# Expert weights in pieces of 2 MB, with runs of 16 KB a partition, in a ring of eight places

## What is computed

```python
x = x + merged(rmsnorm(x, g_mix)) @ w_out            # HGRN2 and pooling, gated; 14 column chunks of w_in
h = rmsnorm(x, g_ffn)
logits = h @ w_router + b_router                     # 32 experts, the top 4 of each token
for e in range(32):                                  # for the tokens sent to expert e
    gate = min(h_e @ w_gate[e] + b_gate[e], 7)
    up = clip(h_e @ w_up[e] + b_up[e], -7, 7)
    y_e = ((up + 1) * gate * sigmoid(1.702 * gate)) @ w_down[e] + b_down[e]
x = x + sum over the experts of weight * y_e
x = x + sigmoid(rmsnorm(x, g_ple) @ w_ple_gate) * (p @ w_ple_proj)
y = rmsnorm(x, g_final)
```

## Time and profile before

| what | value |
|---|---|
| median of three runs | 1386.6 us (1386.1 to 1389.21) |
| the profiled execution's own time | 1386.59 us |
| its span, first to last instruction | 1384.9 us |
| mean granted TensorE clock | 0.982 of full speed |
| PE busy | 1331.2 us (96%) |
| PEld busy | 621.5 us (45%) |
| DVE, ACT, POOL busy | 332.9, 186.4 and 68.3 us |
| DMA queue of SyncE | 442.56 MB (of 10^6 bytes), 77.9% of 16 engines |
| expert pieces issued | 3 x 128, 1024 KB each |

### The profile page before, as it was taken

One profiled execution on the slowest core, in us unless ns is written; L12 is line 12 of the kernel. 1 busy time (PEld: TensorE's weight loads), 2 busy tenths in 40 slices (PEclk: granted clock), 3 DMA queues, 4 the chain that ended last, 5 costly groups with the idle time before them and its releaser, 6 DMA issues.

```text
span 1384.9 us, 15843 instructions
## 1 busy us (share of the span) xinstructions
PE 1331.2 (96%) x6272; PEld 621.5 (45%) x6272; DVE 332.9 (24%) x633; ACT 186.4 (13%) x359; POOL 68.3 (5%) x145
## 2 busy tenths in 40 slices
PE   6999999999899999999999999999999999999995
PEld 5754557364434334343443434434344343434342
DVE  2423424122411221212212122121221212221133
ACT  3314311112111000110001000010000100100022
POOL 7021120030000000000000000000000000000000
PEclk9999999999789999999999999999999999999998
DMA  9743272252559999999999999999999999999920
GB/s 335 264 134 123 61 281 114 62 223 88 215 232 421 421 422 422 421 422 422 422 422 422 422 422 422 422 422 422 422 422 422 422 422 422 422 422 422 420 116 32
DMA packets 79264, 458.70 MB, mean 331 GB/s; under 512 B 8457, under 2 KB 9633, under 8 KB 30080
## 3 DMA queue, kind: packets, MB, share of 16 engines
q1 hardware_dynamic: 73376, 442.56, 77.9%
q0 software_dynamic: 4448, 14.98, 3.5%
q10 hardware_dynamic: 1408, 0.73, 0.2%
HBM read 452.35 MB, written 6.35 MB: 331 GB/s over the span
## 4 chain that ended last, share of the span: by engine, by line
PE 82%; DMA 10%; SPq 3%; DVE 3%; ACT 1%; issue 1%; POOL 0%; ACTq 0%; DVEq 0%
PE bank L965 39%; PE bank L629 10%; PE bank L930 10%; DMA arena<-in_w_up_dram 10%; PE bank L822 4%; PE bank L670 3%; PE bank L1006 3%; SPq L426 3%; PE bank L652 1%; PE bank L742 1%; PE bank L759 1%; PE bank L981 1%; DVE arena L1592 1%; PE bank L939 1%; PE bank L1010 1%; PE bank L598 1%
## 5 line engine op out<-in xcount | busy, mean ns | idle before, releaser
L965 PE MATMUL bank<-arena 128*64 128x512 f32 x3072 | 669.3, 594 | 12.1 <-DVE arena L1592 6.4
L965 PEld LDWEIGHTS bank<-arena 128*64 128x64 f32 x3072 | 226.2, 137 | 442.2 <-issue 438.3
L930 PE MATMUL bank<-arena 128*128 128x128 f32 (+1 forms) x816 | 157.3, 323 | 0.0
L629 PE MATMUL bank<-arena 128*128 128x512 f32 x320 | 144.2, 604 | 0.0
L930 PEld LDWEIGHTS bank<-arena 128*128 128x128 f32 (+1 forms) x816 | 120.6, 201 | 45.4 <-issue 18.0
L629 PEld LDWEIGHTS bank<-arena 128*128 128x128 f32 x320 | 59.8, 192 | 74.3 <-issue 73.5
L1600 DVE TENSOR_TENSOR arena<-bank,arena 128x512 f32<-128x512 f32 (+1 forms) x96 | 61.5, 682 | 96.3 <-PE bank L1006 96.1
L1578 DVE TENSOR_SCALAR arena<-bank 128x512 f32<-128x512 f32 x32 | 20.6, 686 | 195.4 <-PE bank L965 195.4
L1594 DVE COPY arena<-bank 128x512 f32<-128x512 f32 x16 | 11.1, 692 | 217.0 <-PE bank L965 217.0
L670 PE MATMUL bank<-arena 128*128 128x264 f32 x256 | 59.1, 395 | 3.2 <-DVE arena L1328 2.6
L1584 DVE TENSOR_SCALAR arena<-bank 128x512 f32<-128x512 f32 x32 | 20.6, 686 | 168.5 <-PE bank L965 168.5
(11 more groups left out here) (234 smaller groups left out, 736.9 us busy)
## 6 DMA issues: line engine op xcount, KB each, us to landing
arena<-in_w_gate_dram SPq DMA_DIRECT2D x128, 1024.0 KB, 25.5
arena<-in_w_up_dram SPq DMA_DIRECT2D x128, 1024.0 KB, 25.4
arena<-in_w_down_dram SPq DMA_DIRECT2D x128, 1024.0 KB, 21.4
arena<-in_w_in_dram SPq DMA_DIRECT2D x14, 2048.0 KB, 11.5
out_dram<-arena POOLq DMA_DIRECT2D x11, 512.0 KB, 3.8
arena<-in_state_hgrn_dram POOLq DMA_DIRECT2D x8, 512.0 KB, 14.8
arena<-in_w_out_dram SPq DMA_DIRECT2D x4, 1024.0 KB, 14.4
arena<-in_w_ple_gate_dram SPq DMA_DIRECT2D x4, 1024.0 KB, 26.3
```

Source lines behind the costliest of these rows:

```text
L629: ins = pe.matmul(job_bank(name)[:, :], hT[:, k, toks(t)], w[:, k, :], start=(k == 0), stop=(k == KD - 1))
L930: ins = pe.matmul(XG[c][:, (k % 4) * P:(k % 4 + 1) * P], h2[lanes(t), t, every_other(k)], oh[lanes(t), t, :], start=(t == 0), stop=(t == N ...
L965: ins = pe.matmul(out[c][hp(one), :], src[:, k * P + CAP * one:k * P + CAP * one + CAP], w[one][:, j, halves(c)], start=(first and k == 0) ...
```

## The change

A piece becomes half of a matrix, 512 rows, 2 MB. A partition holds four neighbouring rows of the matrix, one run of 16 KB. The ring has eight places and covers the same 16 MB of SBUF. A pair has 12 pieces. A step of `products` waits for two pieces of 2 MB and runs 16 matmuls (32 passes); it frees its places at its end. The slices of `h2` and of the activation have step 4 (16 bytes). Before the loop `granule_used` is counted up by every second `dT` product (4) and by 4 transposes of `h2T`. `w_ple_gate` comes in two loads of 2 MB, still with runs of 4 KB. The diff, cut to its core:

```diff
-GRAN = 2048
+GRAN = 4096
 NGRAN = 3 * D * D // (P * GRAN)
-RING = 16
+RING = 8
...
         gran = [view(R + g * GRAN if g < NGRAN else HG + (g - NGRAN) * GRAN, GRAN).rearrange(
-            "p (j n) -> p j n", j=2) for g in range(RING)]
+            "p (j n) -> p j n", j=4) for g in range(RING)]
...
-            parts = [w.rearrange("o e (g p j) n -> (o e) g p j n", j=2, p=P) for w in (w_gate, w_up, w_down)]
-            ple = w_ple_gate[0].rearrange("(g j p) n -> g p j n", j=2, p=P)
+            parts = [w.rearrange("o e (g p j) n -> (o e) g p j n", j=4, p=P) for w in (w_gate, w_up, w_down)]
+            ple = w_ple_gate[0].rearrange("(g j p) n -> g p j n", j=4, p=P)
...
                     for m in range(3):
-                        for g in range(4):
+                        for g in range(2):
                             for one in range(2):
-                                at_ = 2 * NGRAN * n + 8 * m + 2 * g + one
+                                at_ = 2 * NGRAN * n + 4 * m + 2 * g + one
...
-                pe.matmul(o[:, 0:144], u[:, 0, cc], band0[g], start=True, stop=True, skip_group_check=True).then_inc(s_used, 1)
+                ins = pe.matmul(o[:, 0:144], u[:, 0, cc], band0[g], start=True, stop=True, skip_group_check=True)
+                if c % 2 == 0:
+                    ins.then_inc(s_used, 1)
...
-            turn_rows("h2T", h2, h2_ready, n_used=7, tiles=(2,))
-            turn_rows("h2T", h2, h2_ready, n_used=1, tiles=(0,))
+            turn_rows("h2T", h2, h2_ready, n_used=4, tiles=(2,))
+            turn_rows("h2T", h2, h2_ready, tiles=(0,))
...
             def every_other(k):
-                first = 2 * P * (k // 2) + k % 2
-                return slice(first, first + 2 * P - 1, 2)
+                first = 4 * P * (k // 4) + k % 4
+                return slice(first, first + 4 * P - 3, 4)
...
-                    for g in range(4):
-                        if m == 2 and g % 2 == 0:
-                            pe.wait_ge(s_aTs, 2 * i + g // 2 + 1)
-                        if m == 0 and g == 2:
+                    for g in range(2):
+                        if m == 2:
+                            pe.wait_ge(s_aTs, 2 * i + g + 1)
+                        if m == 0 and g == 1:
                             pe.wait_ge(s_xe, 2 * i + 2)
                         w = list(granules(m, g))
-                        for j in range(2):
-                            k = 2 * g + j
+                        for j in range(4):
+                            k = 4 * g + j
...
-                                    if j == 1 and c == 1 and not (g == 3 and one == 1):
+                                    if j == 3 and c == 1 and not (g == 1 and one == 1):
                                         ins.then_inc(s_used, 1)
```

More of the change, by code:

```diff
@@ L225, in build @@
         wpool = view(G12, 2048).rearrange("p (g k n) -> p g k n", g=4, k=2)
-        wout = view(R + 8 * GRAN, 8192).rearrange("p (k n) -> p k n", k=KD)
+        wout = view(R + 4 * GRAN, 8192).rearrange("p (k n) -> p k n", k=KD)
         band0 = [view(BAND + g * 144, 144) for g in range(4)]
@@ L442, in _ @@
                 load_experts(PER * q, 2 * PER * q)
-            sp.wait_ge(s_used, NGRAN * NE + 4)
+            sp.wait_ge(s_used, NGRAN * NE + 2)
             load_ple()
@@ L446, in _ @@
             with sp.If(more > 0):
-                sp.wait_ge(ld["ple"], 64)
+                sp.wait_ge(ld["ple"], 32)
                 with sp.Fori(1, NBLK) as b:
@@ L450, in _ @@
                         load_experts(b * PAIRS + PER * q, 2 * PER * q)
-                sp.wait_ge(s_used, NGRAN * NE * NBLK + 4)
+                sp.wait_ge(s_used, NGRAN * NE * NBLK + 2)
                 load_ple()
@@ L808, in weights @@
             def weights(w, k, half):
-                return gran[k // 2][:, k % 2, halves(half)] if w is None else w[:, k, halves(half)]
+                return gran[k // 4][:, k % 4, halves(half)] if w is None else w[:, k, halves(half)]
             def quarter(w, k, n):
-                return gran[k // 2][:, k % 2, cols(2, n)] if w is None else w[:, k, cols(2, n)]
+                return gran[k // 4][:, k % 4, cols(2, n)] if w is None else w[:, k, cols(2, n)]
             def product(tag, t, src, w, slices=KD):
@@ L948, in granules @@
                     for one in range(2):
-                        turn, place = divmod(2 * NGRAN * n + 8 * m + 2 * g + one, RING)
+                        turn, place = divmod(2 * NGRAN * n + 4 * m + 2 * g + one, RING)
                         pe.wait_ge(s_gr[place], i0 * (16 * 2 * NGRAN // RING) + 16 * (turn + 1))
@@ L1032, in _ @@
                             pair(b * PAIRS + PER * q, n)
-                pe.wait_ge(ld["ple"], 128)
+                pe.wait_ge(ld["ple"], 64)
             keep_warm(8, Y[1])
@@ L1038, in _ @@
             turn_rows("h3T", h3, lambda t: (s_rows, t + 7))
-            pe.wait_ge(ld["ple"], 64)
+            pe.wait_ge(ld["ple"], 32)
             for t in range(NT):
```

## The result

The changed kernel takes 1544.65 us (median of four runs, 1541.79 to 1546.61) against 1386.6 us for the kernel before (median of three runs, 1386.1 to 1389.21); the ratio of the means is 1.1133, 95% interval 1.1105 to 1.116. A fourth run of the kernel before took 2835.38 us and is left out of these figures. The profiled execution took 1541.79 us, span 1540.0, mean granted clock 0.907 instead of 0.982. The forecast was 1486 us with a range up to 1498, so it had the sign and the place, and was 58.7 us too low.

A forecast was written before the change was run, and what follows sets the result against it. TensorE was taken to set the pace until the ring's lead is eaten, then the weight stream. Kernel before 1386.6, slower loads +105.9 and +1.1, stream waits -7.0: 1486.6 us; full price of the step 1465 to 1498, range 1400 to 1498.

The forecast's parts named there:

- What bounds the kernel, and the place: In the loop, TensorE at 64.7 us a pair outlasts the stream's 59.6 and no longer waits for weights.
- The price of the gather's load: In the gather, a weight load with a step of 16 bytes takes 236 ns instead of 118; chance 0.68.
- The rival with 177 ns: Partial price: a load takes half as much again, a pair 61.4 us, the kernel 1433 us; chance 0.14.
- the upper bound: Each 16 bytes of SBUF touched has its own price: 236 ns a gather load, against a lower bound of 118.
- The transposes' term: The 8 transposes of a pair: each load grows from 120 to 240 ns, adding 8 x 0.120 us a pair.
- the forecast 2.1: Sign of being right: the row of 8 transposes grows from 1.2 to 2.1 us.
- the sum: Kernel before 1386.6, plus 105.9 for 16 pairs, 1.1 for gathers before the loop, less 7.0 of stream waits: 1486.6 us.
- The coarse pieces: First release and last landing each cost 3.5 us, +7.0 us where the stream sets the end; hidden in the forecast.
- The stream's rate: Runs of 16 KB move weights at 428 GB/s instead of 422, 58.8 us a pair; no effect on the forecast time.
- The rule on lines of 16 bytes: SBUF reads need two hits on a 16-byte line; by it the old step is free, the new one not; no price given.
- C: Theory of the follow-up runs, not the prediction: the clock falls because the slow gather gives the array too little work.

The follow-up runs named there:

- step4_turn: The kernel before with step 4 (16 bytes) in the 8 transposes of a pair alone, the gather keeping step 2; 1388.94 us.
- pieces2mb_step2: The changed kernel with each 2 MB piece as two runs of 8 KB a partition, so the slices keep step 2; 1394.73 us.
- narrow32: The kernel before, step 2, with each gather load followed by 32 columns instead of 128; 1402.86 us.
- no8_long: The changed kernel, its gather without the 8 sample rows and with each remaining load and product twice (32 passes of 128 rows); 1476.81 us.
- rows64: The changed kernel with 64 rows instead of 8 in the short passes of the gather; 1539.7 us.
- grouped8: The changed kernel with the gather's loops exchanged, so two changes of row count in a gather instead of eight; 1478.16 us.
- fill256: The changed kernel with each gather load followed by 256 columns instead of 128; 1537.93 us.
- contig_2mb: The changed kernel, but VectorE writes h2 and the activation sorted by slice, so every load is contiguous; 1383.77 us.
- contig_2mb_grouped: The kernel contig_2mb with the gather's loops exchanged as in grouped8, all outputs computed; 1371.16 us.

## Why the prediction missed

**What bounds the kernel, and the place: right.** TensorE sets the end, the gather is what grew, and no products wait for DMA in the loop.

**The price of the gather's load: right.** 233 ns measured for 236 forecast, 48 x (0.233 - 0.118) = 5.5 us a pair. The rival with 177 ns has fallen. The working had luck, though. It chose the upper bound by the single loads of the transposes (140 ns contiguous, 209 with 8 bytes), and just those do not follow it: they stay at 209 ns where I forecast 330.

**The transposes' term (8 x 0.120 = 0.96 us a pair): wrong.** At full clock it is nothing (1.23 us for 1.22, `step4_turn`). The 1.98 us in the changed kernel, which look like the forecast 2.1, are the lower clock. A sign that agrees in size can have another cause; the window's granted clock (0.50) tells them apart.

**The failed step is the sum** "1386.6 + 105.9 + 1.1 - 7.0 = 1486.6 us": it took every duration beside the loads as it was before, at full clock, and put the clock at nothing without a reason. By the rows, a pair grew by 2.97 + 3.08 (gathers), 0.76 (transposes), 1.53 (down) and 2.04 (mix), less 0.3 us of a wait before down that is gone: 10.1 us, of which 5.5 are loads and 4.6 the clock, for 6.62 us in the sum. 1379.6 + 16 x 10.11 + 1.0 (the loop starts at 391.98, before at 390.98) = 1542.4 us; the profiled execution took 1541.79. The view was there: with half the clock in the gathers before the loop I had a stretch of the same instructions at 0.50, and did not ask whether the same could happen in the loop once its loads got slower.

**The coarse pieces: right.** Forecast 1393.6 for them alone, measured 1394.73. SyncE's queue issues the first freed pieces at this time:

```profile
401.82 8.06 SPq L426 DMA_DIRECT2D arena<-in_w_down_dram  x4
```

401.82 for 397.42: 3.5 us for the step, as forecast, and 0.9 more since the loop starts 1.0 later (forecast 1.1, from the slower loads of the two gathers before it). In `pieces2mb_step2` the same issue is at 400.90, as forecast.

**The stream's rate: right.** 428 GB/s forecast, 429 measured where the stream bounds. It could not act here, as forecast.

**The rule on lines of 16 bytes.** The gather's prices at steps of 8, 12, 16 and 32 bytes fit lines of 16 bytes, the last by costing no more than the third. The Trainium skill (Advanced Engine Details and Errata, Memory Cachelines) says that SBUF has lines of 16 bytes, that at least two hits on a line are needed to absorb the latency of an access, and that a new line for each access costs. The gather agrees: 110 ns contiguous, 118 with two hits, 233 with one. The transposes disagree: two hits a line already take 209 ns for 140, and one hit a line takes no more than two.

**Shown and open.** Shown: the loss is the step alone; a bit more than half is the loads, the rest the clock; the clock falls without loads of 16 bytes step (`narrow32`) and holds with them at the same length when all passes have 128 rows (`no8_long`); it holds with the eight changes when the loads are fast (kernel before). So with 128 columns behind each load it takes the slow loads and the short passes with their changes together. Supported: the changes weigh more than the few rows (`rows64`). Open: whether the change itself does it or the time that it adds. A wider form of C would be that slow loads, few columns and changes act alike, since each means fewer columns in the same time. It fits `narrow32`, `no8_long` and `rows64`; but `grouped8` (24 passes in 5.99 us) and `no8_long` (32 in 7.57) are close to each other in it and differ in the clock, so no run here decides on it. Open too: what lets the clock fall in some gathers of `grouped8` and `fill256` and not in others of the same kernel, and why the transposes escape the price.

## What to carry over

A weight layout that puts j rows in one run of a partition sets the step of the other operand. Before taking it, count the 16-byte stretches that LDWEIGHTS will touch, and sort the rows by slice where VectorE writes them anyway. When a stretch of small loads gets slower, forecast the clock of what stands behind it too, with rows of the same instructions at the lower clock as the price. Put products with few rows together, and not one behind every second product: each change of row count costs 0.19 us here.

## What the hardware showed unexpectedly

- A load of 128 x 128 before a pass of a two-pass product comes every (0.52 - 0.189) / 3 = 110 ns contiguous (`contig_2mb`), 118, 173, 233 and 232 ns at steps of 8, 12, 16 and 32 bytes.
- A single load before a one-pass transpose lasts 140 ns contiguous, 209 with a step of 8 bytes, 209 with 16.
- Exchanging two loops, with the same passes, takes 1.16 us off a gather at full clock (4.22 to 3.06), 0.19 for each of the six changes less, and half of the two gathers before the loop, 15.06 to 7.83 us, where the clock comes back within them: the window 376 to 384 has 0.50 in `contig_2mb` and 1.00 in `contig_2mb_grouped`.
- Behind a wait of 2.59 us for a piece, in the loop of `contig_2mb_grouped`, 32 passes of up take 8.62 us at a granted clock of 0.82; behind a wait of 1.31 us they take 7.09.
- Runs of 4, 8 and 16 KB a partition move 410, 422 and 429 GB/s.
